# One decoder step with a gated recurrence: sample states laid out sample by sample, and one vector operation ahead of a wait

## The reference

```python
# per head: q, k, f (T, 128), v (T, 128); S is (128 keys, 128 values)
S_t = diag(f_t) @ S_{t-1} + outer(k_t, v_t)      # the recurrence
o_t = S_t.T @ q_t
# samples: one step each, from state_hgrn[0, sample, head]
S_new = f[:, None] * S_old + k[:, None] * v[None, :]
o     = S_new.T @ q
# then o is normalised per head, gated with silu(g), multiplied by w_out and added to h
```

## Time and profile before

| what | value |
|---|---|
| device time, median of 3 executions | 985.9 us (985.83 to 986.24) |
| span of the profiled execution | 984.2 us |
| PE busy | 962.7 us, 98% |
| PE weight loads busy | 902.2 us, 92% |
| DVE, ACT, POOL busy | 577.2, 380.9, 406.1 us |
| granted TensorE clock, mean | 0.994 |

### The profile page before, as it was taken

The page is one execution under the profiler, slowest core; times in us unless marked ns, Lnnn a source line. Parts: engine busy times, 40 slices in busy tenths (PEclk is TensorE's granted clock), DMA queues, the critical chain, the costliest instruction groups (busy, mean ns, idle before and its releaser), DMA issues.

```text
span 984.2 us, 23595 instructions
## 1 busy us (share of the span) xinstructions
PE 962.7 (98%) x9958; PEld 902.2 (92%) x9958; DVE 577.2 (59%) x1195; ACT 380.9 (39%) x766; POOL 406.1 (41%) x295
## 2 busy tenths in 40 slices
PE   6999999999999999999999999999999999999996
PEld 6989999999999999899999999999998888788896
DVE  6455555555464645656942234456667857977635
ACT  7521322231313133424432223442127767866423
POOL 2265455454536363512225541441104534445343
PEclk9999999999999999999999999999999989999999
DMA  9521222223131312332324422321112222332104
GB/s 362 181 66 54 82 69 66 78 58 92 43 111 26 110 45 91 111 110 66 135 80 151 156 88 82 117 66 59 49 43 82 71 65 78 120 101 73 47 30 144
DMA packets 52921, 89.96 MB, mean 91 GB/s; under 512 B 15720, under 2 KB 34760, under 8 KB 52688
## 3 DMA queue, kind: packets, MB, share of 16 engines
q1 hardware_dynamic: 52528, 88.10, 27.9%
q10 hardware_dynamic: 288, 0.35, 0.1%
HBM read 70.80 MB, written 17.64 MB: 90 GB/s over the span
## 4 chain that ended last, share of the span: by engine, by line
PE 92%; DMA 3%; DVE 1%; SPq 1%; ACT 1%; issue 1%; POOL 0%; DVEq 0%; ACTq 0%
PE G L1657 64%; PE G L1954 9%; PE R L1716 3%; PE R L1885 2%; PE R L1899 2%; DMA ST<-xs 2%; PE R L1738 1%; PE R L1727 1%; PE R L1919 1%; PE R L1741 1%; PE R L1929 1%; PE R L1657 1%; PE R L1688 1%; PE R L1747 1%; DMA FG<-head_scales 1%
## 5 line engine op out<-in xcount | busy, mean ns | idle before, releaser
L1657 PE MATMUL G<-XH,WH 128*128 128x344 f32 x1160 | 377.4, 328 | 7.9 <-ACT XH L915 7.9
L1657 PE MATMUL G<-XL,WH 128*128 128x344 f32 x1160 | 370.3, 322 | 1.5 <-DVE XL L1285 0.8
L1657 PE MATMUL G<-XH,WL 128*128 128x344 f32 x744 | 235.6, 320 | 0.0
L1657 PEld LDWEIGHTS G<-XH,WH 128*128 128x128 f32 x1160 | 218.3, 189 | 16.2 <-issue 12.8
L1657 PEld LDWEIGHTS G<-XL,WH 128*128 128x128 f32 x1160 | 218.1, 189 | 4.6 <-issue 3.2
L682 POOL TENSOR_TENSOR WL<-WR,WH 128x1024 fp32r<-128x1024 f32 x40 | 103.3, 2582 | 159.8 <-ACT WH L826 159.8
L1657 PEld LDWEIGHTS G<-XH,WL 128*128 128x128 f32 x744 | 139.7, 188 | 0.0
L1657 PE MATMUL G<-XL,WL 128*128 128x344 f32 x416 | 133.3, 320 | 0.0
L826 ACT ACTIVATE WH<-WR 128x1024 fp32r<-128x1024 f32 x58 | 61.2, 1056 | 182.8 <-PE G L1657 156.7
L713 POOL TENSOR_TENSOR K<-K,FP 128x512 f32<-128x512 f32 x48 | 76.7, 1597 | 91.1 <-PE R L1716 91.1
L759 POOL TENSOR_TENSOR SP<-SP,small 128x1024 f32<-128x1024 f32 (+1 forms) x32 | 57.2, 1787 | 115.1 <-DVE small L1506 115.1
(11 more groups left out here) (272 smaller groups left out, 1719.2 us busy)
## 6 DMA issues: line engine op xcount, KB each, us to landing
WR<-w SPq DMA_DIRECT2D x58, 512.0 KB, 3.8
A<-x SPq DMA_DIRECT2D x8, 516.0 KB, 7.3
FG<-head_scales SPq DMA_DIRECT2D x8, 516.0 KB, 3.6
RESO<-x SPq DMA_DIRECT2D x8, 516.0 KB, 4.7
h_spill<-H SPq DMA_DIRECT2D x8, 516.0 KB, 2.9
gate_spill<-EV SPq DMA_DIRECT2D x24, 172.0 KB, 2.0
RES<-h_spill SPq DMA_DIRECT2D x24, 172.0 KB, 2.8
SS<-states SPq DMA_DIRECT2D x8, 512.0 KB, 5.4
```

The costliest lines, as they stand in the source:

```text
L1657: return nc.tensor.matmul(U[unit_bank(NU * n + i)][:, 0:TU], w[:, n % 3, k, :], x[:, seg(i)], start=(k == 0 and p == 0), stop=(k == KT - 1 ...
```

## The change

The eight states of a head lie in `SS` as [key, value, sample] before and as [key, sample, value] after, so that the 128 values of one sample are contiguous. All that touches them follows: the scratch tensor in memory for the sample values is [sample, value], it is written with a transposing transfer and read back as before, in the new order; the views in `decode_parts`, `decode_state` and `decode_add` are turned over; the matmul of group OS streams `SS[:, n]`; and the inputs and outputs of the kernel have the new order already in memory. The other edit moves the wait for O1 in `first_query` behind the multiplication of the odd queries.

```diff
@@ -138,7 +138,7 @@
     x_d, w_d, gain_d, lbl_d, st_d, lmask_d, imask_d, ident_d, cs_d, amask_d, smask_d, sink_d, sinks_d, kc_d, vc_d, xt_d, xs_d = ins
     y_d, stp_d, sts_d, kwin_d, vwin_d = outs
     h1_d = nc.dram_tensor("h1_spill", [P, KT, T], fp32, kind="Internal").ap()
-    vs_d = nc.dram_tensor("sample_values", [HEADS, P, DEC], fp32, kind="Internal").ap()
+    vs_d = nc.dram_tensor("sample_values", [HEADS, DEC, P], fp32, kind="Internal").ap()
     rn_d = nc.dram_tensor("head_scales", [HEADS, 4, TQ], fp32, kind="Internal").ap()
     os_d = nc.dram_tensor("sample_outputs", [HEADS, DEC, P], fp32, kind="Internal").ap()
     sg_d = nc.dram_tensor("gate_spill", [P, HP, T], fp32, kind="Internal").ap()
@@ -187,7 +187,7 @@
     AT = sb("AT", [P, NC, P], fp32, ra)
     VH = sb("VH", [P, NC, P], fp32, ra)
     ST = sb("ST", [P, NC, P], fp32, ra)
-    SS = sb("SS", [P, P, DEC], fp32, ra)
+    SS = sb("SS", [P, DEC, P], fp32, ra)
     QDEC = sb("QDEC", [P, 2, DEC], fp32, ra)
     DECC = sb("DECC", [P, 2, NC + DEC], fp32, ra)
     lmask = sb("lmask", [P, NL, P // 2], u8, ra)
@@ -508,11 +508,11 @@
         def sample_values(r):
 
             sp.wait_ge(unit_read, 9 * r + 9)
-            sp.dma_start(vs_d[r], RAWV[:, SEQ:T]).then_inc(vs_out, 16)
+            sp.dma_start(vs_d[r].rearrange("b e -> e b"), RAWV[:, SEQ:T], allow_slow_non_contiguous=True).then_inc(vs_out, 16)
             if r:
                 sp.wait_ge(ss_prod, 2 * r)
             sp.wait_ge(vs_out, 16 * (r + 1))
-            sp.dma_start(VD[:, 0:SEQ], vs_d[r].rearrange("e b -> (e b)").unsqueeze(0).broadcast_to([P, SEQ])
+            sp.dma_start(VD[:, 0:SEQ], vs_d[r].rearrange("b e -> (b e)").unsqueeze(0).broadcast_to([P, SEQ])
                          ).then_inc(vd_in, 16)
 
         def sample_outputs(p):
@@ -716,7 +716,7 @@
         def decode_parts(r):
             pool.wait_ge(ss_in, 16 * (r + 1))
             pool.wait_ge(fp_done, r + 1)
-            nc.gpsimd.tensor_tensor(SS[:], SS[:], DECC[:, r % 2, NC:].unsqueeze(1).broadcast_to([P, P, DEC]), ALU.mult
+            nc.gpsimd.tensor_tensor(SS[:], SS[:], DECC[:, r % 2, NC:].unsqueeze(2).broadcast_to([P, DEC, P]), ALU.mult
                                     ).then_inc(ss_decayed, 1)
 
         for n in range(2):
@@ -1201,11 +1201,11 @@
 
             dve.wait_ge(f_done, r + 1)
             dve.wait_ge(q_done, r + 1)
-            if r:
-                dve.wait_ge(group_done, group_value(r - 1, "O1"))
             odd = QM[:, :, 32:48]
             gates = FG[:, 0:SEQ].rearrange("p (c n two) -> p c n two", n=16, two=2)
             nc.vector.tensor_tensor(odd, QM[:, :, 1:32:2], gates[:, :, :, 1], ALU.mult).then_inc(q1_done, 1)
+            if r:
+                dve.wait_ge(group_done, group_value(r - 1, "O1"))
             qu = QU[:].rearrange("p (c n two) -> p c n two", n=16, two=2)
             nc.vector.tensor_tensor(qu[:, :, :, 0], QM[:, :, 0:32:2], gates[:, :, :, 0], ALU.mult)
             dve.wait_ge(q1_done, r + 1)
@@ -1234,15 +1234,16 @@
             for i in range(2):
                 dve.wait_ge(vd_in, 16 * (r + 1))
                 dve.wait_ge(k_done, r + 1)
-                nc.vector.tensor_tensor(VK[:, half(i)].rearrange("p (e b) -> p e b", b=DEC),
-                                        VD[:, half(i)].rearrange("p (e b) -> p e b", b=DEC),
-                                        K[r % 2][:, SEQ:T].unsqueeze(1).broadcast_to([P, 64, DEC]),
+                own = K[r % 2][:, SEQ + 4 * i:SEQ + 4 * i + 4]
+                nc.vector.tensor_tensor(VK[:, half(i)].rearrange("p (b e) -> p b e", b=4),
+                                        VD[:, half(i)].rearrange("p (b e) -> p b e", b=4),
+                                        own.unsqueeze(2).broadcast_to([P, 4, P]),
                                         ALU.mult).then_inc(ss_prod, 1)
 
         def decode_add(r):
             dve.wait_ge(ss_prod, 2 * r + 2)
             dve.wait_ge(ss_decayed, r + 1)
-            nc.vector.tensor_tensor(SS[:], SS[:], VK[:, 0:SEQ].rearrange("p (e b) -> p e b", b=DEC), ALU.add
+            nc.vector.tensor_tensor(SS[:], SS[:], VK[:, 0:SEQ].rearrange("p (b e) -> p b e", b=DEC), ALU.add
                                     ).then_inc(ss_done, 1)
 
         def chunk_states(r):
@@ -1745,7 +1746,7 @@
             for n in range(DEC):
                 j, v = divmod(n, 4)
                 ins = nc.tensor.matmul(b[32 * v:32 * v + 32, j * P:(j + 1) * P],
-                                       QDEC[:, r % 2, n:n + 1].broadcast_to([P, 32]), SS[:, :, n], start=True, stop=True)
+                                       QDEC[:, r % 2, n:n + 1].broadcast_to([P, 32]), SS[:, n], start=True, stop=True)
             ins.then_inc(group_done, 1)
 
         def head_sums(m):
@@ -2071,7 +2072,7 @@
     sk = v["b_sinks"][0][pair]
     arrays = {
         "x": features_first(x), "w": w, "gains": gains, "lbl": v["a_lb_logits"][0].reshape(HEADS, P).T,
-        "states": v["state_hgrn"][0].transpose(1, 2, 3, 0), "lmask": lmask.reshape(P, -1),
+        "states": v["state_hgrn"][0].transpose(1, 2, 0, 3), "lmask": lmask.reshape(P, -1),
         "imask": np.eye(P, dtype=np.uint8), "ident": np.eye(P, dtype=f), "cs": cs, "amask": amask, "smask": smask,
         "sink": np.broadcast_to(sk, (P, 16)), "sinks": np.tile(v["b_sinks"][0], DEC)[:, None],
         "kc": v["cache_k_win"].transpose(2, 3, 0, 1).reshape(P, DEC, P),
@@ -2080,7 +2081,7 @@
     arrays["xt"] = v["x_prompt"][0].reshape(NC, P, D).transpose(1, 0, 2)
     arrays["xs"] = v["x_sample"][:, 0]
     arrays = {k: np.ascontiguousarray(a) for k, a in arrays.items()}
-    outs = {"y": (P, KT, T), "stp": (HEADS, P, P), "sts": (HEADS, P, P, DEC), "kwin": (P, P + DEC),
+    outs = {"y": (P, KT, T), "stp": (HEADS, P, P), "sts": (HEADS, P, DEC, P), "kwin": (P, P + DEC),
             "vwin": (P, P + DEC)}
     nc = bacc.Bacc("TRN2", target_bir_lowering=False, num_devices=1)
     ins = [nc.dram_tensor(k, a.shape, mybir.dt.from_np(a.dtype), kind="ExternalInput").ap() for k, a in arrays.items()]
@@ -2090,5 +2091,5 @@
     got = run_bass_kernel_spmd(nc, [arrays], core_ids=[0]).results[0]
     y = got["y"].transpose(2, 1, 0).reshape(T, D)
     kw, vw = (got[n].reshape(2, 64, P + DEC).transpose(2, 0, 1) for n in ("kwin", "vwin"))
-    return (y[:SEQ][None], y[SEQ:][:, None], got["stp"][None, None], got["sts"].transpose(3, 0, 1, 2)[None],
+    return (y[:SEQ][None], y[SEQ:][:, None], got["stp"][None, None], got["sts"].transpose(2, 0, 1, 3)[None],
             kw[:P][None], vw[:P][None], kw[P:][:, None], vw[P:][:, None])
```

## The result

The changed kernel takes 1018.4 us (median of 5 executions, 1014.4 to 1021.8), beside 985.9 us for the kernel before (5 executions, 985.7 to 987.6). The ratio is 1.033, with a 95% interval of 1.031 to 1.035: slower by 32.5 us, where 3.8 us of gain were forecast.

The account below looks back on a forecast made before the run. PE was taken to bound the kernel, working at full clock in nearly every slice. Eight heads at 0.47 us sum to 3.8 us, other terms adding nothing: 985.9 - 3.8 = 982.1 us, range 980.5 to 984.0.

Parts of the forecast that it names:

- The stride and the move: Group OS on PE: contiguous operand cuts 1.04 to 0.57 us a head; without moving the wait, seven heads gain about 0.05.
- Rival A: Stride is not the cause: OS stays at 1.04 us, move worth at most 0.05 a head, 985.5 us; chance 0.08.
- line 1208 would end more than 2 us before OS: Moved ahead of the wait for O1, this DVE operation fills idle time and ends over 2 us before OS begins.
- DVE's and POOL's terms: DVE's repeated key costs nothing; POOL's line 719 shortens by 0.5 us a head, off the path, valued at nothing.
- the margin at D3: Last quarter of the diagonal needs a bank ACT empties of O1; next thing to be late, by 0.3 us.
- Transfers: Sample-value write becomes 1024 single 4-byte values: 0 to +2 us, value +1, priced from the transposing read of `A`.
- as long as SP has slack: SP's queue absorbs the longer write: next duty 15 us later in passes 2 to 7, 2.5 us slack in pass 8.
- rival C: Element-wise write holds SP up in pass 8, `head_scale(0)` and all behind; a 16 us write gives 988; chance 0.03.
- The rule that I weighed and set aside: Non-contiguous last dimension makes one descriptor per element, eight times as many for the write; sum held at 3.8 us given slack.

Follow-up runs that it names:

- e1_old_write: Changed kernel with sample values written and read back in the old order (128 runs of 32 bytes), DVE turning them over: 981.1 us, ratio 0.995.
- e5_own_lines: Changed kernel with each of the 1024 written values 64 bytes from the next; read-back takes an input row instead: 980.7 us, ratio 0.995.
- e13_extra_dense: e1_old_write plus one packed element-wise write of 1024 values in each head, read by nobody, in the recurrence: 1032.7 us, ratio 1.048.
- e14_extra_sparse: Experiment 13: e1_old_write plus the same eight unread packed writes, placed in the output projection behind the stores to `h_spill`: 998.2 us, ratio 1.013.
- experiments 1, 2, 5 and 12: 1 is e1_old_write, 5 is e5_own_lines, 12 is e13_extra_dense; 2 is the kernel before with the element-wise write alone: 1025.7 us, ratio 1.040.
- experiment 11: Changed kernel with SP issuing the 512 KB load of `states` right behind the element-wise write, before waiting for it: 1030.8 us, ratio 1.045.

## Why the prediction was wrong, and where it was right

**The stride and the move: right.** OS was to take the price of line 1755, and it does: 0.57 us, with 273 ns for one instruction against 275 foreseen. Rival A falls. The Trainium skill's rule on 16-byte lines (page "SBUF — State Buffer", section "Door 1: The DMA port swizzle") agrees in sign, by 411 and 273 ns; its threshold was not measured. The move is what makes it count, as said: alone, layout and move bring 0.7 and 0.8 us, together 4.7. That is 0.9 more than the sum, and most of it stands in the piece behind OS, which the sum left alone: the diagonal costs 0.68 us in place of 0.78, 0.7 in seven heads. The forecast for all this was 982.1 us; e1_old_write, which is the change without the write, takes 981.1, inside the range on record. That line 1208 would end more than 2 us before OS was a slip: by the earlier trace rows it is 336.85 - 2.86 + 0.70 = 334.69, 1.95 us before, and nothing hangs on it. DVE's and POOL's terms were right at nothing, and so was the margin at D3, where no new wait appeared.

**Transfers: the step that failed.** The term was "0 to +2 us, with +1 as my value" for the write, off the path, with a price from the transposing read of `A`. Measured, SP's wait from issue to read-back has a median of 11.5 us in place of 3.9 to 4.0, so about +7.5. The row compared as many elements, but of the other direction: single values read out of memory still land after 2.3 us in the changed kernel, while single values packed into memory need five times as long. I named the direction and did not let it widen the bound. That was one error.

The other was larger. The text said that the sum stays 3.8 "as long as SP has slack", and rival C priced a slow write only through SP's queue in pass 8, with a cost from 6 us more on, and a kernel slower than before from 12. By that reckoning +7.5 us would have cost about 1.5 us, and the kernel would still have been faster. A slow transfer was thought to hurt only those that wait for it. But other transfers beside it land late (the states after 12.1 us in place of 6.1, `h_spill` after 12.3 in place of 3.0), PE's signals to POOL and DVE come up to 6.4 us late, and PE loses 19.1 us in idle time in passes 1 to 8, with nothing in the program waiting for the write except SP. Rival C had the right culprit and sign, and the wrong mechanism, place and size; its chance of 0.03 was a judgement on that mechanism alone.

**The rule that I weighed and set aside** had the right sign. The Trainium skill, page "DMA: Bandwidth & Descriptors", section "Rules for kernel authors", warns of one descriptor for each element. But that is not the price here: e5_own_lines has the same 1024 elements and costs 1 us more on the write and nothing in time. The same page, section "Specifications", says that transfers below 512 B are done by read-modify-write. That fits the table in part, since the writes that share 64 bytes are the slow ones. It doesn't give the whole, since values 64 bytes apart are below 512 B as well and are quick.

**Where the 37 us are.** The profiled executions of the changed kernel and of e1_old_write have spans of 1012.6 and 979.3, 33.3 apart. 19.1 are idle time of PE that the profile gives no reason for, 9.2 of them waits for POOL. The mean clock is 0.984 against 0.994, which is 0.010 x 1012.6 = 10.1 us; the four spells at the lower level, 20.4 us at half the clock, come to the same. Some 4 us I can't assign; missing matmul records and short pieces of idle time by ACT and DVE would be in it. The medians are 37.4 apart, as the profiled execution was the quickest of the five.

**What stops PE: half of it shown, the rest open.** Shown is that a signal of PE that others wait for comes 2 to 8 us late while such a write is under way in the recurrence, and that this chain (PE to POOL and back to PE) gives 9.2 of 19.1 us in the changed kernel and 15.4 of 31.7 in e13_extra_dense. Why the signal is late, and what holds PE in the middle of a unit, no run shows. One theory was that PE lacks instructions. They are loaded by DMA too, and the queues of the changed kernel are (packets, MB, share of 16 engines):

```profile
q8 instruction: 79, 1.29, 0.6%
...
q14 instruction: 26, 0.21, 0.1%
```

Together 1.50 MB for 23595 instructions, 64 bytes each. By the Trainium skill, page "Perfetto Trace Analysis", section "The 4-stage abstract model", an instruction is 64 bytes, and the trace agrees. PE has 9958 matmuls and as many weight loads, which makes 1.27 MB, so q8 with its 79 packets is PE's: 16 KB or 256 instructions in a packet. Those last 256 / 28 = 9 us in the recurrence and 256 / 13 = 20 us in the output projection. If PE had no more than one packet in reserve, which no run shows, a hold of some 10 us would let it run dry in the first and not in the second, and that would fit e13_extra_dense (31.7 us) and e14_extra_sparse (none that is new).

The raw records speak for it in part and against it in more. For it: three of q8's packets in the changed kernel, at 105.5, 205.3 and 412.3 us, take 3.3 to 3.75 us where others need about 1, and PE has idle pieces close to each. Against it: in pass 6 PE has four pieces between 310 and 315 us, while q8's packets land at 306.35 and the next starts at 317.33; in e13_extra_dense the longest piece ends at 168.49, with no packet of q8 between 160.03 and 172.90. A lack of instructions should end when a packet lands. And the late signals belong to matmuls that PE has already run. So the loading of instructions is not shown, and can't be the whole.

A rival that no run tests is the recording itself. Every execution timed here has a recorded span and clock. In the stretch where signals are late, the trace also lacks records: of the 113 updates of the semaphore of DVE's merges it has 103 in the changed kernel and 92 in e13_extra_dense, and all 113 in the kernel before, in e1_old_write and in e14_extra_sparse. Whether PE would stand as long without a recording is open. That the packed write is what sets all this off is shown either way, by experiments 1, 2, 5 and 12.

Of experiment 13 the time was missed (998 us, above the expectation): I had thought only of PE's own instructions and not of the other transfers of that stretch, though experiment 11 had just shown them to be held. The same error twice.

Open is how the waiting arises in memory; the rows show only that 16 single writes to 64 bytes are slow. Whether runs of 16 bytes would be as quick as 32 was not tried.

## What to carry to other kernels

Price a transfer by its direction and by how its pieces fall in memory, and not by its count of elements: pieces of a few bytes, packed side by side and written from many partitions, are to be avoided even where nobody waits for them. Let the reader of the data do the turning, as DVE's view does here at no cost, or leave gaps. And where a rival is a slow transfer, price what else is under way during it: the other transfers, and each handover between engines. Where the profile calls idle time "issue" or "remote", take the waits from the program, and compare when the engine waited for had finished with when the waiting one starts: the difference from a good run is where the time went.

## What the chip showed that I had not expected

- 1024 packed values of 4 bytes take 11.5 us to be written, 128 of them still 9.3; 1024 values 64 bytes apart take 5. Reading 1024 single values takes 2.3 us.
- While such a write is under way, a load of 512 KB lands after 12.1 us in place of 6.1, and a store of 516 KB that was issued before it after 12.3 in place of 3.0.
- While such a write is under way in the recurrence, POOL starts up to 6.4 us after the matmul whose signal it waits for (8.1 in e13_extra_dense), in place of 0.1. PE then stands for up to 3.4 us in one piece (4.4 in e13_extra_dense), and after one such piece it was granted 0.60 of its clock over the next 7.2 us.
- A streamed fp32 operand with a stride of 32 bytes takes 411 ns for 128 columns and a contiguous one 273.
